# Eight expert layers streamed through one core: two-tile rounds in a loop against one-tile rounds in straight line

## The reference, cut to what matters

```
def moe(x, w_router_l, wg, wu, wd):
    logits = (x @ w_router_l).astype(jnp.float32)
    top_v, top_i = lax.top_k(logits, TOP_K)
    gates = jax.nn.softmax(top_v, axis=-1)
    combine = jnp.sum(jax.nn.one_hot(top_i, N_EXPERTS) * gates[..., None], axis=-2)
    for e in range(N_EXPERTS):
        out = out + combine[..., e:e + 1] * swiglu(x, wg[e], wu[e], wd[e])
```

## Time and profile before

| | us |
|---|---|
| median of 3 runs | 2135.48 (2134.16 to 2135.63) |
| span of the profiled execution | 2131.6 |
| experts, first product to last | 1085.94 to about 2098.4 |
| TensorE busy over the span | 1916.8 (90%) |
| VectorE busy | 909.3 (43%) |
| ScalarE busy | 675.0 (32%) |

### The profile page before, as it was taken

How to read it: one execution, slowest core, us unless ns; L and a number is a source line. 1 busy time by engine, 2 the same in 40 slices (tenths; PEclk the granted TensorE clock), 3 DMA queues, 4 the chain that set the end, 5 groups by cost and what they waited for, 6 DMA issues and landing times.

```text
span 2131.6 us, 20882 instructions
## 1 busy us (share of the span) xinstructions
PE 1916.8 (90%) x7660; PEld 1289.0 (60%) x7661; DVE 909.3 (43%) x1352; ACT 675.0 (32%) x1026; POOL 109.5 (5%) x93
## 2 busy tenths in 40 slices
PE   6999898899996798999779898989999898999793
PEld 2444444788886796554656565656666566666562
DVE  0303602433335724442545555555555544333454
ACT  1103211433324222221234444444444443221342
POOL 2111110000000500000010000000000000000001
PEclk9999998999998897557679999999999999999897
DMA  9565659333334423001559999999999997544792
GB/s 298 188 214 182 198 203 358 121 119 119 99 119 93 125 80 99 1 1 59 178 173 303 324 325 314 333 315 313 307 326 301 322 299 261 178 148 159 235 297 110
DMA packets 359072, 436.78 MB, mean 205 GB/s; under 512 B 32332, under 2 KB 311528, under 8 KB 358968
## 3 DMA queue, kind: packets, MB, share of 16 engines
q1 hardware_dynamic: 334160, 397.44, 57.4%
q10 hardware_dynamic: 20456, 25.21, 3.4%
q0 software_dynamic: 4352, 12.88, 1.7%
HBM read 417.57 MB, written 17.93 MB: 204 GB/s over the span
## 4 chain that ended last, share of the span: by engine, by line
PE 81%; DVE 9%; issue 5%; ACTq 2%; ACT 2%; DMA 1%; DVEq 0%; POOL 0%; POOLq 0%
PE ps L1601 33%; PE ps L1618 15%; PE ps L1525 7%; PE ps L1566 5%; PE ps L1498 4%; PE ps L1629 4%; PE ps L1668 3%; PE ps L1731 3%; PE ps L1707 2%; DVE split L1219 2%; PE ps L1580 2%; PE ps L1680 2%; ACTq L821 2%; DVE ring_split L1283 1%; DVE extra_split L1283 1%
## 5 line engine op out<-in xcount | busy, mean ns | idle before, releaser
L1601 PE MATMUL ps<-split,hi_x 128*128 128x512 f32 (+1 forms) x2304 | 693.4, 386 | 25.0 <-issue 20.2
L1219 DVE TENSOR_TENSOR split<-ring,split 128x1024 fp32r<-128x1024 f32 (+1 forms) x432 | 469.1, 1131 | 103.3 <-ACT split L829 101.4
L1601 PEld LDWEIGHTS ps<-split,hi_x 128*128 128x128 f32 x2304 | 419.8, 193 | 110.6 <-issue 33.2
L1601 PE MATMUL ps<-split,lo_x 128*128 128x512 f32 (+1 forms) x1152 | 438.8, 381 | 0.0
L829 ACT ACTIVATE split<-ring 128x1024 fp32r<-128x1024 f32 (+1 forms) x432 | 389.3, 977 | 52.7 <-issue 35.2
L1618 PE MATMUL ps<-ring,work 128*128 128x512 f32 x792 | 357.9, 593 | 3.7 <-DVE work L1252 3.7
L857 ACT ACTIVATE work<-ps 128x256 f32<-128x256 f32 (+1 forms) x144 | 52.8, 367 | 691.8 <-PE ps L1601 691.7
L1246 DVE TENSOR_TENSOR work<-work,ps 128x256 f32<-128x256 f32 (+1 forms) x144 | 57.4, 399 | 479.1 <-ACT work L857 432.1
L1601 PEld LDWEIGHTS ps<-split,lo_x 128*128 128x128 f32 x1152 | 220.8, 192 | 42.1
L1618 PEld LDWEIGHTS ps<-ring,work 128*128 128x128 f32 x792 | 147.9, 189 | 150.6 <-issue 142.8
L1525 PE MATMUL ps<-ring,cond 128*2 128x256 f32 x576 | 128.0, 383 | 9.6 <-DMA ring<-in_w_mod_dram 9.6
(11 more groups left out here) (219 smaller groups left out, 1575.7 us busy)
## 6 DMA issues: line engine op xcount, KB each, us to landing
ring<-in_moe_w_gate_dram SPq DMA_DIRECT2D x80, 1024.0 KB, 7.4
ring<-in_moe_w_up_dram SPq DMA_DIRECT2D x80, 1024.0 KB, 9.9
ring<-in_moe_w_down_dram SPq DMA_DIRECT2D x80, 1024.0 KB, 5.1
ring<-in_w_mod_dram SPq DMA_DIRECT2D x36, 1024.0 KB, 7.4
mod_extra<-in_w_mod_dram SPq DMA_DIRECT2D x12, 1024.0 KB, 6.9
ring<-in_w_qkv_dram SPq DMA_DIRECT2D x6, 2048.0 KB, 8.9
ring<-in_w_in_dram SPq DMA_DIRECT2D x5, 2048.0 KB, 10.3
ring<-in_ffn_w_gate_dram SPq DMA_DIRECT2D x10, 1024.0 KB, 7.7
```

The source lines that it names most:

```text
L1219: dve.tensor_tensor(low, raw, high.bitcast(F32), ALU.subtract).then_inc(lo_ok, 1)
L1601: ins = pe.matmul(ps[:, 0, 0:2 * w], xt(c_), split[:, j % 2, part, c_, 0:2 * w], start=(c_ == 0 and n == 0), stop=(c_ == KC - 1 and n == 2))
```

## The change

The FFN and attention keep their code. Their buffers and those of the experts are placed in one arena, and the experts are rewritten:

1. **Rounds of one tile.** Eight rounds, one per expert, as straight-line code with constant counts. Token rows beyond 128 go to further rounds of one tile, up to five, in a loop behind them, each loading its expert's weights again. With this case's inputs there is one.
2. **512-wide blocks.** The hidden width is five blocks of 512 and one of 256. Gate and up are separate chunks and separate products into banks 0 and 1; a down piece is a chunk too. A chunk is 16 KB a partition (2 MB).
3. **Ring of chunks.** Six raw slots and three slots for high parts; the low part overwrites the raw chunk in place. A chunk is loaded once PE has used the chunk six before it (`w_used`); high parts are split two chunks ahead of PE.
4. **The down product is split too**, three fast passes, with the turned hidden rows split by ACT and DVE as well.
5. **Routing.** The first expert's indices are read after two one-hot groups (`idx_first`), so that the first gather starts then; the list of further rounds and the places of the results are computed by DVE inside round 0 (`further_rounds`, `places`).
6. **Zeroing** shrinks to one transfer of 2.6 MB. `w_o` loads wait for the value products and go to two chunk slots.

The core of the diff:

```
+BLOCK = 512
+BLOCKS = [BLOCK] * 5 + [D_FF - 5 * BLOCK]
+RAW, HIGH = 6, 3
+MORE = 5
+ORDER = [("gate", 0), ("up", 0), ("gate", 1), ("up", 1), ("down", 0), ("gate", 2), ("up", 2), ("down", 1),
+         ("gate", 3), ("up", 3), ("down", 2), ("gate", 4), ("up", 4), ("down", 3), ("gate", 5), ("up", 5),
+         ("down", 4), ("down", 5)]
...
+            for r in range(EXPERTS):                       # SP
+                for c_ in range(CHUNKS):
+                    n = r * CHUNKS + c_
...
+                    elif n >= RAW:
+                        sp.wait_ge(w_used, n - RAW + 1)
+                    load_chunk(r, c_)
...
+            def w_split_high(r, c_):                       # ACT
+                act.wait_ge(w_full[c_ % RAW], of_round(r, 16 * (CHUNKS // RAW), 16 * (c_ // RAW + 1)))
+                if not isinstance(r, int) or r * CHUNKS + c_ >= HIGH:
+                    act.wait_ge(w_used, of_round(r, CHUNKS, c_ - HIGH + 1))
+                for n in range(PIECES_OF[c_]):
+                    act.activation(piece(w_high, c_ % HIGH, n), piece(w_raw, c_ % RAW, n), ACT.Copy).then_inc(w_high_ok, 1)
...
+            def expert_round(r):                           # DVE
+                for c_, (kind, b) in enumerate(ORDER):
+                    if c_ and ORDER[c_ - 1][0] == "up":
+                        hid(r, ORDER[c_ - 1][1])
+                    if kind == "up" and b:
+                        hid_low(r, b - 1)
+                    if c_ == CHUNKS - 1:
+                        hid_low(r, b)
+                        tokens_in(of_round(r, 1, 2))
+                    if c_ + 2 < CHUNKS:
+                        w_split_low(r, c_ + 2)
+                    else:
+                        w_split_low(r + 1, c_ + 2 - CHUNKS)
+                    if isinstance(r, int) and r == 0 and c_ == 3:
+                        further_rounds()
+                    if isinstance(r, int) and r == 0 and c_ == 9:
+                        places()
...
+            def into_hidden(r, b, kind, bank):             # PE
+                for k in range(KC):
+                    if k * w % D == 0:
+                        split_in(r, c_, k * w // D)
+                    for n, (xt, wt) in enumerate(((xg_hi, wh), (xg_hi, wl), (xg_lo, wh))):
+                        ins = pe.matmul(ps[:, bank, 0:w], xt[:, k, :], wt[:, k, :],
+                                        start=(k == 0 and n == 0), stop=(k == KC - 1 and n == 2))
+                ins.then_inc(w_used, 1)
...
+                    else:
+                        if c_ == CHUNKS - 1:
+                            turn_hid(r, b)
+                            turn_tokens(of_round(r, 16, 32))
+                        out_of_hidden(r, b)
...
+            for r in range(EXPERTS):
+                expert_round(r)
+            pe.wait_ge(more_ok, 1)
+            rounds = pe.value_load(over[0:1, 20:21], min_val=EXPERTS, max_val=EXPERTS + MORE)
+            with pe.Fori(EXPERTS, rounds) as i:
+                expert_round(i)
```

More of the change, by code:

```diff
@@ L539, in _ @@
[L539 to L562, removed]
@@ new lines, in expert_of @@
+            def expert_of(i):
+                return sp.value_load(over[0:1, i], min_val=0, max_val=EXPERTS - 1)
+            sp.wait_ge(more_ok, 1)
+            rounds = sp.value_load(over[0:1, 20:21], min_val=EXPERTS, max_val=EXPERTS + MORE)
+            e = expert_of(slice(EXPERTS, EXPERTS + 1))
+            for c_ in range(2):
+                sp.wait_ge(w_used, EXPERTS * CHUNKS + c_ - RAW + 1)
+                load_chunk(e, c_)
+            with sp.Fori(EXPERTS, rounds) as i:
+                e = expert_of(bass.ds(i, 1))
+                for c_ in range(2, CHUNKS):
+                    sp.wait_ge(w_used, of_round(i, CHUNKS, c_ - RAW + 1))
+                    sp.sem_inc(chunk_free, 1)
+                    load_chunk(e, c_)
+                e = expert_of(bass.ds(i + 1, 1))
+                for c_ in range(2):
+                    sp.wait_ge(w_used, of_round(i, CHUNKS, CHUNKS + c_ - RAW + 1))
+                    sp.sem_inc(chunk_free, 1)
+                    load_chunk(e, c_)
@@ L637, in _, with gather @@
[L637 to L642, removed]
-                    pool.wait_ge(gathered[k], i * 16 + 16)
-                    pool.wait_ge(xg_turned[k], i + 1)
-                    gather(k, bass.ds(i + 1, 1))
-                    pool.wait_ge(idx_ok[k], i + 2)
-                    pool.sem_inc(gather_go, 1)
-                    gather_rows(k)
+            def gather(col, count):
+                pool.tensor_copy(idx_now[:, :], idx_tab[:, col]).then_inc(idx_ok, 1)
+                pool.wait_ge(idx_ok, count)
+                if not isinstance(count, int):
+                    pool.sem_inc(gather_go, 1)
+                pool.indirect_dma_start(
+                    out=xg[:, :], out_offset=None, in_=hn_rows,
+                    in_offset=bass.IndirectOffsetOnAxis(ap=idx_now[:, 0:1], axis=0),
+                ).then_inc(gathered, 16)
@@ L651, in _ @@
+            gather_next(EXPERTS - 1)
+            rounds = pool.value_load(over[0:1, 20:21], min_val=EXPERTS, max_val=EXPERTS + MORE)
+            with pool.Fori(EXPERTS, rounds) as i:
+                gather_next(i)
             pool.wait_ge(rounds_over, 1)
@@ L1478, in _ @@
+            tokens_in(1)
+            for r in range(EXPERTS):
+                expert_round(r)
+            rounds = dve.value_load(over[0:1, 20:21], min_val=EXPERTS, max_val=EXPERTS + MORE)
+            with dve.Fori(EXPERTS, rounds) as i:
+                expert_round(i)
             dve.wait_ge(gb_ok, 32 * 4)
@@ new lines, in expert_round @@
+            def expert_round(r):
+                first = isinstance(r, int) and r == 0
+                pe.wait_ge(xg_dve, of_round(r, 1, 1))
+                for c_, (kind, b) in enumerate(ORDER):
+                    if kind == "gate":
+                        if b or not first:
+                            pe.wait_ge(gate_act, of_round(r, N_BLOCKS, b))
+                        into_hidden(r, b, "gate", 0)
+                    elif kind == "up":
+                        if b:
+                            turn_hid(r, b - 1)
+                        elif not first:
+                            pe.wait_ge(hid_ok, of_round(r, N_BLOCKS, 0))
+                        into_hidden(r, b, "up", 1)
+                    else:
+                        if b == 0 and not first:
+                            pe.wait_ge(y_d, of_round(r, 1, 0))
+                            pe.wait_ge(y_a, of_round(r, 1, 0))
+                        if c_ == CHUNKS - 1:
+                            turn_hid(r, b)
+                            turn_tokens(of_round(r, 16, 32))
+                        out_of_hidden(r, b)
```

594 lines of the change are left out of this document (287 added, 307 removed).

## The result

The changed kernel takes 1977.1 us, median of 4 runs (1976.13 to 1978.16), against 2135.35 of 4 runs of the kernel before on the same chip: a ratio of 0.926, with a 95% interval of 0.9247 to 0.9273. The forecast was 1990, its own range 1975 to 2004. The other 2 us of the difference come from the 3.9 us that the forecast added to get from span to median, which is 1.6 us here.

A forecast was written before the change was run, and what follows sets the result against it. PE and transfers were both near their end in the experts' one-tile rounds. First product 1076.0, cold passes 1.65, nine rounds 869.2, loop entry 3, tail 33.2 + 3.2 gave 1986.3, forecast 1990 us; own range 1975 to 2004, whole 1972 to 2045.

The forecast's parts named there:

- the step from span to median: From the summed profile span, 1986.3 us, to the median of runs: 3.9 us added, giving 1990.
- The bound: Experts' rounds after the change: PE at 95.55 us sets the round, transfers at 92.7 us are 3% under it.
- The round, 96.7: One expert round of one tile: 95.55 us of PE work plus 1.1 us charged at its end.
- The bubble: Round's end: DVE reaches the last hidden low part late, 1.1 us of PE a round, bounds 0 and 4.6.
- Loop entry, 3 us: Entering the loop of the ninth round, with a register load: 3 us of PE, bounds 0 and 8.32.
- The first product, 1076.0: Routing's end: the earlier gather brings the first expert product near 1076.0 instead of 1085.94, bounds 1071 and 1086.
- zeroing: ACT's queue, held 33.89 us before: hidden behind PE's output product, so nothing, bound 1 us of gain.
- The end: After PE's end: the store comes about 4.4 us later, 3.2 more than before; the remaining 33.2 us of tail stay.
- Transfers bind: Rival in the experts' rounds: at 348 GB/s a round is 102.4 us and the total 2041; chance 0.20.
- Engines late: Rival at eight round ends: the 8.32 us gap comes back, 66 us, total 2056; chance 0.11.
- Slower: Rival: a ninth round at today's pace, total 2135 or 2154; today's pace or worse 0.07, of which slower 0.05.
- the loop's jump: Round's end of the kernel before: PE's 8.32 us wait goes with no jump, no choice, no table reload.

The follow-up runs named there:

- two passes: The changed kernel without the third pass of every expert product (X_low W_high, in gate, up and down), transfers and splits kept: 1926.85 us.

## Why the prediction held, point by point

The mechanism was right, and the time lies 2 us above the lower end of the range because most of the terms that were off were too high: the round, the loop's entry, the first product, and the step from span to median.

**The bound.** PE sets the round, with transfers behind it by a narrow margin: right, and shown by two passes. I gave 3% (92.7 against 95.55); it is 4% of PE's work (90.9 against 94.93).

**The round, 96.7.** It is 95.88. PE's work is 94.93 instead of 95.55, since a block of 512 takes 17.00 (1295.17 to 1312.17) and not 17.16. The bubble is 0.95 instead of 1.1; the late low part at the round's last block was foreseen, the one a block earlier was not. Together 7 us of the 10.8 by which the sum was too high.

**Loop entry, 3 us.** Nothing: from the first expert product of the round ahead of the loop (1746.72) to that of the looped round (1842.60) PE takes 95.88, as in the others. The bound of 8.32 came from the earlier trace rows, a round's end with a choice in it, so the nearest row was one of something else.

**The first product, 1076.0.** 1073.75. The steps were as told: index products end at 1067.4, tokens behind the second chunk. Of the 2.25 us, 1.4 are an earlier start of the index products (1056.74 instead of 1058.17), which lies within what the start varies between runs; that zeroing costs or gains less than 1 us could not be separated from that.

**The end.** Store 4.2 us after PE's end, told 4.4; tail 36.4, as told.

**The rivals.** *Transfers bind* fell, but it takes only the old row size or one slot less for them to show. *Engines late* fell for straight-line code, and would have been the outcome for a loop with a choice: 53 us more, told as 66. *Slower* fell because the 0.96 share was not full, as two passes show with 1.05 at 392 GB/s.

**Where the gain came from.** Of the 147.2 us in the experts the split down product gives 51, measured. The rest is the round's end, where one-tile rounds lost 114.90 - 11 x 9.19 - 0.88 = 12.9 us each before. The choice put back into the new kernel costs 6.7 a round, 53 in all. Windows from the first expert product to PE's end show what this is made of: before, after, with the choice, and with the unsplit down product.

```profile
1085.94:2098.40 1012.46, 942.54 (x3654) 642.13 (x3654) 498.07 (x618) 392.13 (x518) 22.36 (x30) 0.97 0.83 273
1073.75:1939.03 865.28, 857.77 (x4050) 709.83 (x4050) 761.34 (x758) 635.41 (x725) 9.25 (x16) 1.00 0.98 362
1071.20:1990.32 919.12, 874.88 (x4050) 719.00 (x4050) 761.34 (x759) 637.00 (x725) 9.21 (x16) 0.98 0.93 340
1075.01:1992.11 917.10, 916.84 (x3654) 636.57 (x3654) 505.08 (x505) 446.78 (x527) 9.21 (x16) 1.00 0.92 341
```

PE's idle time, length less busy time, falls from 69.9 us to 7.5. Its busy time falls by 84.8: by 59.1 for the split down product (916.84 to 857.77), which brings some 7 us of idle time with it, and by 25.7 more. The granted clock is a part of these, with a mean of 0.97 before and 1.00 now; how large a part I did not separate from small differences between the steps. Two rows of the kernel before: a window around the wait of the earlier trace rows, in which the clock stood at the lower of its two levels (1.2 GHz), and PE's longest wait, ahead of the last round, where the two-tile copy ends and the other follows:

```profile
1430.30:1440.50 10.20, 5.32 (x14) 4.27 (x15) 5.29 (x6) 2.61 (x3) 0.00 (x0) 0.50 1.07 372
...
1991.79 1.21 PE L1601 MATMUL ps<-split,hi_x 128*128 128x512 f32 x2 [13.35 <-issue]
```

With the choice put back PE runs the same 4050 products, stands idle 36.7 us longer and is busy 17.1 us longer, at 0.98: the choice costs the waits and slower passes behind them. The shares of the old body's other parts I did not separate: it has two more choices a round on ACT and DVE (`left > 1`), and another order. The prediction charged the round's end to "the loop's jump" with the choice and the table reload; the jump back is the part that costs nothing. Its sum also took every pass at the full clock, behind the first cold ones, without saying so; rounds at 1.00 bore that out.

## What to carry to other kernels

Before unrolling a loop, look at the instruction queues of the DMA view: where they were silent inside the loop here, its jump cost nothing to be measured, and the choice between two copies of a long body was what to remove. A DMA share of 1.0 does not say that transfers bind; ask whether anyone waits for one, take work from the busy engine, and see at what rate the rounds then run. And when an engine splits ahead for the next stage, put what the current stage still waits for between the pieces: three such moves gave 13.6 us here.

## What the runs showed of the hardware

A choice between two copies of a round made DVE idle 8.4 to 10.1 us at a round's end, where a plain loop has 2.2, and cost a round 6.7 us; the jump back alone left rounds at 95.89 to 95.92 us against 95.88, and a register load cost nothing to be measured. Of the choice's cost over eight rounds, 17 us were the same products at a mean granted clock of 0.98 instead of 1.00. One core alone moved 392 GB/s for 700 us, with most rows of 2 and 4 KB, and 368 with gate and up in rows of 1 KB. A gather of 0.5 MB was used 5.1 us after its issue with no weight chunk beside it, and 8.1 us after with one of 2 MB.
